# Two prompt tiles of a PEER layer taken through the whole expert table by matrix products, in place of gathered rows

## What is computed

```python
q = (hb @ w_q).reshape(PEER_BLOCK, PEER_HEADS, 2, PEER_KEY_DIM // 2)
# top 16 of 128 on each half, top 16 of their sums: 8 heads x 16 experts e of 16384
gate = jax.nn.softmax(top_s, axis=-1)
act = jax.nn.gelu(jnp.einsum('thkd,td->thk', u_tab[e], hb), approximate=False)
return jnp.einsum('thk,thkd->td', gate * act, v_tab[e])
```

## Time and profile before

| | us |
|---|---|
| median of 3 runs | 3367.15 (3362.72 to 3370.08) |
| span of the profiled execution | 3372.4 |
| TensorE busy | 2967.9 |
| VectorE busy | 2247.2 |
| ScalarE busy | 1569.5 |
| GpSimd busy | 1299.0 |

### The profile page before, as it was taken

One profiled execution on the slowest core, in us unless ns is written; L12 is line 12 of the kernel. 1 busy time (PEld: TensorE's weight loads), 2 busy tenths in 40 slices (PEclk: granted clock), 3 DMA queues, 4 the chain that ended last, 5 costly groups with the idle time before them and its releaser, 6 DMA issues.

```text
span 3372.4 us, 34890 instructions
## 1 busy us (share of the span) xinstructions
PE 2967.9 (88%) x10654; PEld 1563.0 (46%) x10654; DVE 2247.2 (67%) x5353; ACT 1569.5 (47%) x4312; POOL 1299.0 (39%) x1097
## 2 busy tenths in 40 slices
PE   7988899988999898989898888998897988798877
PEld 5764556653445444554454333443353434353322
DVE  1268737685678647884779568866777486873854
ACT  2137334555456334643456345644563454432433
POOL 0023324344344434443434444453334443343532
PEclk8998999999999999999999999999999998899999
DMA  4279999999999999999999999999999989999998
GB/s 175 91 298 362 387 386 396 418 394 421 421 420 411 421 422 419 393 405 422 421 400 413 421 422 421 410 421 422 396 382 408 422 351 333 353 393 369 421 422 342
DMA packets 241250, 1298.74 MB, mean 385 GB/s; under 512 B 46068, under 2 KB 70804, under 8 KB 100646
## 3 DMA queue, kind: packets, MB, share of 16 engines
q0 software_dynamic: 156672, 1140.92, 82.5%
q1 hardware_dynamic: 84390, 155.59, 12.4%
HBM read 1279.41 MB, written 16.44 MB: 384 GB/s over the span
## 4 chain that ended last, share of the span: by engine, by line
PE 44%; DMA 28%; DVE 20%; ACT 4%; issue 2%; SPq 1%; POOL 0%; DVEq 0%; ACTq 0%
PE PS L1096 21%; DMA R<-in_t_uv,idx 18%; DVE R L1746 8%; PE PS L779 7%; DMA R<-in_t_uv,idxS 4%; DMA wring<-in_w_out 3%; PE PS L745 2%; PE PS L1018 2%; PE PS L860 2%; PE PS L859 2%; DVE xb L1757 2%; DMA wring<-in_w_query 2%; PE PS L1045 2%; DVE SC L1712 1%; DVE SC L1709 1%
## 5 line engine op out<-in xcount | busy, mean ns | idle before, releaser
L1096 PE MATMUL PS<-R,diag 128*128 128x512 f32 x3776 | 1821.4, 619 | 200.3 <-ACT diag L1378 173.6
L710 POOL DMA_INDIRECT R<-in_t_uv,idx x1024 | 1234.3, 1205 | 1949.1 <-PE PS L1096 1389.3
L1746 DVE CUSTOM_DVE_ANT_0 R<-R,hb 128x1024 f32<-128x1024 f32 x1088 | 1315.7, 1220 | 726.4 <-DMA R<-in_t_uv,idx 645.3
L1096 PEld LDWEIGHTS PS<-R,diag 128*128 128x128 f32 x3776 | 694.6, 195 | 1077.5 <-issue 635.4
L1369 ACT ACTIVATE acts<-dots 128x1 f32<-128x1 f32 x1088 | 217.2, 200 | 1103.1 <-DVE dots L1746 1100.4
L1378 ACT ACTIVATE diag<-ident,wv 128x128 f32<-128x128 f32 x880 | 353.7, 402 | 76.9 <-PE PS L1096 49.0
L779 PE MATMUL PS<-R 128*128 128x128 f32 (+2 forms) x2272 | 317.1, 295 | 38.6 <-ACT stg L1140 26.7
L779 PEld LDWEIGHTS PS<-R 128*128 128x128 f32 x2272 | 298.5, 196 | 113.1 <-issue 104.5
L1371 ACT ACTIVATE wv<-gate,acts 128x1 f32<-128x1 f32 x1024 | 301.9, 295 | 33.3
L1757 DVE SCALAR_TENSOR_TENSOR xb<-R,wv,xb 128x1024 f32<-128x1024 f32 x144 | 184.4, 1281 | 1.7 <-ACT wv L1371 1.7
L1018 PE MATMUL PS<-wring,T 128*128 128x512 f32 x256 | 133.0, 649 | 42.6 <-DMA wring<-in_w_out 42.6
(11 more groups left out here) (243 smaller groups left out, 2376.0 us busy)
## 6 DMA issues: line engine op xcount, KB each, us to landing
wring<-in_w_out SPq DMA_DIRECT2D x64, 512.0 KB, 14.0
wring<-in_w_query SPq DMA_DIRECT2D x64, 512.0 KB, 8.1
R<-in_t_win SPq DMA_DIRECT2D x38, 512.0 KB, 8.5
R<-in_t_uv,idx POOLq DMA_INDIRECT x1024, 14.0
R<-in_t_win SPq DMA_DIRECT2D x9, 1024.0 KB, 16.0
pr<-prd SPq DMA_DIRECT2D x8, 976.0 KB, 12.7
prd<-stg SPq DMA_DIRECT2D x54, 128.0 KB, 7.6
xb<-in_x_prompt SPq DMA_DIRECT2D x8, 512.0 KB, 7.9
```

Source lines behind the costliest of these rows:

```text
L710: e.indirect_dma_start(dst, None, table, bass.IndirectOffsetOnAxis(ap=index, axis=0)).then_inc(S[s], c.count(name, s, 16))
L1096: m = mm(bank(n), diag[:, NTH[s] % DR, :], pair(s)[:, D + 512 * n:D + 512 * n + 512], start=begins, stop=s == last_slot(t), skip_group_che ...
L1746: e.tensor_tensor_reduce(u, u, hb[:, tile_of(g) % 2, :], 1.0, 0.0, ALU.mult, ALU.add, dots[:, g % NW:g % NW + 1]).then_inc(dve_done, c.cou ...
```

## The change

Tiles 3 and 5 (`DENSE`) no longer have slots. The remaining tiles go in the order `GO`, 832 slots in all. For the dense tiles:

- `gb` (71 steps over 68 slots, twice): for each token of the tile a 128 x 128 matrix of its gates over all 16,384 experts, out of two one-hot matrices that DVE builds (four operations of 128 columns for two tokens) and PE multiplies; ACT copies it to `g_stage`, SP stores it in DRAM (`spread_g`, 8 stores of 1 MB a tile in pieces of 512 bytes).
- `dn` (264 steps over slots 582 to 826): 64 groups of 256 experts. SP loads u transposed (1 MB), v (1 MB) and a quarter of 1 MB of `spread_g`; PE forms u x h for both dense tiles at once (2 x 8 products of 256 columns), ACT applies gelu, DVE multiplies by the gates, PE adds w x v to four PSUM banks (8 products of 512 columns).
- `kept_x`, `kept_h`: residual and h of the dense tiles, stored and loaded again; `fin` ends the two tiles.

Besides: `on_dve` takes two slots of five, the first six of a tile, and all from slot 560 (`PE_END`) on; the ring has eight buffers, from slot 440 (`NARROW`) on seven; each tile's mixers are laid over 66 slots (`BEGIN`), the whole top-k over 40 of them; the input projections lie beside slots 20 to 76 and 112 to 258; the sample's attention beside 492 to 560. `g_final` is no longer loaded for each tile: PE spreads one row into `Y` (`gfin`). `xb`, `hb`, `idx` and `gate` hold three tiles (`OWN`, `PRIOR`). The sample tile's two halves are added by one product with `fold` at the end.

```diff
-RN = 9
+RN = 8
-WIDE = 4 * P + 38, 6 * P + 8
-NSLOT = NTILE * P + NSMP
+GO = [1, 2, 4, 6, 7, 8, SMP]
+DENSE = [3, 5]
+OWN = {1: 1, 2: 0, 3: 2, 4: 1, 5: 2, 6: 0, 7: 2, 8: 1, 9: 0}
+PRIOR = {4: 1, 5: 3, 6: 2, 7: 5, 8: 4, 9: 6}
+NSLOT = P * (len(GO) - 1) + NSMP
+NARROW = 440
+PE_END = 560
+NGRP = P // 2
 def on_dve(s):
-    return s < P * NTILE and 3 <= s % P < 57 and s % P % 3 == 2
+    return s >= PE_END or s % P < 6 or s % 5 in (1, 3)
 def ring():
-        if s == WIDE[0]:
-            free.extendleft(range(RN, RN + 2))
-        if s == WIDE[1]:
+        if s == NARROW:
             free = deque(i for i in free if 2 * i < SAUX)
+BEGIN = {2: 17, 3: 92, 4: 158, 5: 224, 6: 290, 7: 356, 8: 422, SMP: 492}
 def plan():
-    for n, at, end in ((1, 8, 164), (2, 182, 4 * P + 28)):
+    for n, at, items_at, end in ((1, 6, 20, 76), (2, 96, 112, 258)):
         spread(stage("ldx", n), at, at + 1)
+        spread(prep(n), at + 4, items_at - 4)
+        spread(stage("ldw", n), items_at - 4, items_at - 3)
+        spread(stage("items", n), items_at, end)
+    for t in range(2, SMP):
+        at = BEGIN[t]
+        spread(stage("att", t) + stage("ret", t), at, at + 36)
+        spread(stage("ldb", t), at + 18 if t > 2 else 8, at + 19)
+        spread(tail(t), at + 36, at + 58)
+        spread(top(t, 0) + top(t, 1), at + 58, at + 98)
+        if t > 2:
+            spread(stage("ldr", t), at + 24, at + 25)
+        if t + 1 <= NTILE:
+            spread(stage("lda", t + 1), at + 42, at + 43)
+            spread(stage("kv", t + 1) + stage("q", t + 1), BEGIN[t + 1] - 8, BEGIN[t + 1])
+    for j, at in ((0, 262), (1, 334)):
+        spread(stage("gb", j), at, at + 68)
+    at = BEGIN[SMP]
+    spread(stage("ldc", SMP), at - 24, at - 1)
+    spread(stage("lds", SMP), at - 22, at - 16)
+    spread(stage("kv", SMP) + stage("q", SMP), at - 8, at)
+    spread(stage("atts", SMP) + stage("rets", SMP), at, at + 68)
+    spread(stage("ldr", SMP), at + 50, at + 51)
+    spread(tail(SMP), at + 68, at + 90)
+    spread(top(SMP, 0), at + 90, at + 110)
+    spread(stage("sts", SMP), at + 72, at + 92)
+    spread(stage("dn", 0), at + 90, NSLOT - 6)
+    spread(stage("fin", 0) + stage("fin", 1), NSLOT - 6, NSLOT + LAG)
...
@@ SyncE @@
+            def gb(p, j):
+                for f in range(8):
+                    yield from p.to(5 + 8 * f + 8)
+                    at = 8 * j + f
+                    e.wait_ge(act_done, c.at("act", f"G{j}_{8 * f + 7}"))
+                    dma(spread_g.rearrange("(g p) (c x) -> p g c x", p=P, c=16)[:, :, at, :],
+                        g_stage[f % 2].rearrange("p (g x) -> p g x", g=16), f"gs{f % 2}", f"G{j}_{f}")
+            def load_u(i):
+                if i >= 2:
+                    e.wait_ge(pe_done, c.at("pe", f"dU{i - 2}"))
+                dma(d_u[i % 2], A["t_ut"][P * i:P * i + P, :], f"du{i % 2}", f"u{i}")
+            def load_v(i):
+                if i >= 2:
+                    e.wait_ge(pe_done, c.at("pe", f"dV{i - 2}"))
+                for a in range(2):
+                    dma(d_v[i % 2][a], A["t_uv"][2 * P * i + P * a:2 * P * i + P * a + P, D:2 * D], f"dv{i % 2}", f"v{i}_{a}")
...
@@ TensorE @@
+            def dn(p, t):
+                for k in range(4 * NGRP + 4):
+                    yield from p.to(4 + k)
+                    i, what = k // 4, k % 4
+                    if what % 2 == 0 and i < NGRP:
+                        a = what // 2
...
+                        for q in range(NCH):
+                            m = mm(at, u[:, q, P * a:P * a + P], TB[:, :, P * q:P * q + P], start=q == 0, stop=q == NCH - 1,
+                                   skip_group_check=True)
+                    if what % 2 and i:
+                        i, j = i - 1, what // 2
+                        if j == 0:
+                            e.wait_ge(S[f"dv{i % 2}"], c.at(f"dv{i % 2}", f"v{i}_1"))
+                            e.wait_ge(dve_done, c.at("dve", f"dW{i}"))
+                        for n in range(2):
+                            for a in range(2):
+                                m = mm(bank(4 + 2 * j + n), d_w(i)[:, 2 * P * a + P * j:2 * P * a + P * j + P],
+                                       d_v[i % 2][a][:, 512 * n:512 * n + 512], start=i == 0 and a == 0,
+                                       stop=i == NGRP - 1 and a == 1, skip_group_check=True)
...
@@ ScalarE @@
+            def dn(p, t):
+                for i in range(NGRP):
+                    yield from p.to(4 + 4 * i + 3)
+                    e.wait_ge(pe_done, c.at("pe", f"dU{i}"))
+                    if i >= 4:
+                        e.wait_ge(pe_done, c.at("pe", f"dV{i - 4}"))
+                    act(d_w(i), bank(2 + i % 2), ACT.Gelu).then_inc(act_done, c.count(f"dg{i}"))
...
@@ VectorE, its 64 steps @@
+            def gb(p, j):
+                for n in range(64):
+                    yield from p.to(3 + n)
...
+                    if n >= 2:
+                        e.wait_ge(pe_done, c.at("pe", f"G{j}_{n - 2}"))
+                    for tok in range(2):
+                        m = 2 * n + tok
+                        ts(g_hot(n, tok, 0), iota[:], g_kT[:, P + m:P + m + 1], g_kT[:, 2 * P + m:2 * P + m + 1], ALU.is_equal,
+                           ALU.mult).then_inc(dve_done, c.count())
+                        ts(g_hot(n, tok, 1), iota[:], g_kT[:, m:m + 1], None, ALU.is_equal).then_inc(
+                            dve_done, c.count(f"Gh{j}_{n}" if tok else None))
@@ VectorE @@
+            def dn(p, t):
+                for i in range(NGRP):
+                    yield from p.to(4 + 4 * i + 4)
+                    n = i // 4
+                    if i % 4 == 0:
+                        e.wait_ge(S[f"dg{n % 2}"], c.at(f"dg{n % 2}", f"g{n}"))
+                    e.wait_ge(act_done, c.at("act", f"dg{i}"))
...
+                    tt(w, w, g, ALU.mult).then_inc(dve_done, c.count(f"dW{i}"))
...
@@ VectorE @@
+            def fin(p, j):
+                yield from p.to(0)
+                e.wait_ge(S["dx"], c.at("dx", "x1"))
+                e.wait_ge(pe_done, c.at("pe", f"dV{NGRP - 1}"))
+                tt(d_x[j], two(4 + 2 * j), d_x[j], ALU.add).then_inc(dve_done, c.count(f"sd{j}"))
```

More of the change, by code:

```diff
@@ L88 @@
 NTH = {s: i for q in (BY_PE, BY_DVE) for i, s in enumerate(q)}
+PE_OF = {t: [s for s in BY_PE if tile_of(s) == t] for t in GO}
+SUMMED = [t for t in GO if PE_OF[t]]
 def stage(st, t):
@@ L253, in build @@
         prd = nc.dram_tensor("prd", (SMP * P, IN_W), F32).ap()
+        kept_h = nc.dram_tensor("kept_h", (2 * P, D), F32).ap()
+        kept_x = nc.dram_tensor("kept_x", (2 * P, D), F32).ap()
+        spread_g = nc.dram_tensor("spread_g", (P // 8 * P, 2 * D), F32).ap()
         def bank(b, lo=0, hi=512):
@@ L562, in ldc @@
                     e.wait_ge(*spent(c, max(s for s in wide if s in q)))
+                e.wait_ge(pe_done, c.at("pe", "G1_63"))
+                for f in range(2):
+                    e.wait_ge(S[f"gs{f}"], c.at(f"gs{f}", f"G1_{6 + f}"))
                 st_in = A["state_ret"].rearrange("o b (c a) d e -> (o a) d b c e", a=2)
@@ L667, in peer @@
+            def fin(p, j):
+                yield from p.to(3)
+                t = DENSE[j]
+                e.wait_ge(dve_done, c.at("dve", f"yd{j}"))
+                dma(A["o_yp"][P * (t - 1):P * t, :], d_x[j], "yd", f"y{t}")
             def peer(g):
-                for t in range(1, SMP + 1):
+                for t in GO:
                     if g == last_slot(t) + LAG + 3:
@@ L1100, in _, with gfin @@
+            def gfin(t):
+                for n in range(2):
+                    m = mm(bank(n), ones(n), gfin_half(n), start=True, stop=True)
+                m.then_inc(pe_done, c.count(f"gfin{t}"))
             run(dict(prep=prep, items=items, kv=kv, meta=meta, q=q, att=att, ret=ret, atts=atts, rets=rets, out=out, norm2=norm2,
-                     query=query, quart=quart), peer)
+                     query=query, quart=quart, gb=gb, dn=dn), peer)
         @block.scalar
@@ L1763, in build @@
+            run(dict(prep=prep, kv=kv, meta=meta, q=q, att=att, ret=ret, atts=atts, rets=rets, out=out, norm2=norm2, top=top, gb=gb, dn=dn,
+                     fin=fin), peer)
     return new_marks
```

360 lines of the change are left out of this document (251 added, 109 removed).

## The result

| | before | after |
|---|---|---|
| median, us | 3367.72 (3362.72 to 3370.08) | 3591.13 (3584.77 to 3596.5) |
| span of the profiled execution, us | 3372.4 | 3583.0 |

Ratio 1.0661, 95% interval 1.0638 to 1.0683: 6.6% slower. The forecast was 3395 us in a range of 3220 to 3510: the sign was right (slower had a chance of 0.53), the size and the range were not.

A forecast was written before the change was run, and what follows sets the result against it. The kernel before was taken as DMA-bound after its first 190 us, TensorE following at 88%. For the changed kernel, 2376 us to slot 582, 984 dense and 40 at the end gave 3400 of span, forecast 3395, range 3220 to 3510.

The forecast's parts named there:

- heavy stretches: Seven 40-slot stretches with a tile's whole top-k and most of the next attention: VectorE-bound, 144 us each, 1008 in all.
- light stretches: Five 26-slot stretches between heavy stretches, holding the projections: 84 us each by DMA, 420 us in all.
- margin for a bound by DMA alone: 2% that a DMA-bound tile loses, added to the 2054 us from slot 20 on: 41 us.
- dense part: Slots 582 to 826: DMA-bound, 410 MB in 984 us, TensorE 909 us and 4 to 8% behind.
- second rival: Uncovered hand-offs between TensorE, gelu and VectorE in the dense part, 2 us a group: 1058 not 984, total 3470; chance 0.15.
- the 144: VectorE's time in us for one of the heavy stretches: slot products, top-k, kv, q and most of an attention.
- Building G: 40 steps of four 128-column VectorE operations in each of two heavy stretches, 0.19 us an operation: +60 us for both.
- full ring: Five slots of gathers already held when one of the light stretches begins: 12 us less DMA time there.
- the third rival: Three weight buffers, 14.0 us to land, set the light stretches: +11 to 15 us in seven tiles, total 3490; chance 0.08.
- The sample's attention: Slots 492 to 560: 235 us, between 210 at the engines' pace and 290 with the chain unchanged.
- The first rival: Stretches even out and total DMA time is the bound: 3198 us, partly evened up to 3330; chance 0.33.
- 60 where 40 was the full rate: Writing spread_g in 512-byte pieces, 16.8 MB: 60 us of DMA taken, 40 at full rate, most of it hidden.

The follow-up runs named there:

- the denser kernel before: Kernel before, with attention and retention of tiles 3 to 8 over 36 slots, not 49, and projections over 22, not 44: 3521.47 us, ratio 1.0429.

## Why the prediction was right or wrong

| part | forecast | measured |
|---|---|---|
| to slot 20 | 281 | 277 |
| slots 20 to 75 | 245 | 244 |
| 75 to 115 | 151 | 142 |
| 115 to 150 | 110 | 145 |
| three heavy stretches without G | 432 | 459 |
| two with G | 348 | 374 |
| 480 to 520 | 144 | 177 |
| five light stretches | 420 | 521 |
| 520 to 560 | 134 | 137 |
| 560 to 582 | 70 | 92 |
| margin for a bound by DMA alone | 41 | - |
| dense part, 582 to 826 | 984 | 981 |
| end | 40 | 34 |

**Bytes and counts** held, and so did the **dense part**: 981 us at 418 GB/s against 984, TensorE 909.74 us busy against 909. The second rival (hand-offs there) fell; its stretch was below the forecast's.

**The heavy stretches** held in kind: VectorE 90 to 96% busy over their 40 slots, DMA share 0.76 to 0.84. They came out 5 to 12 us above the 144, and those with G together 26 above 348. Building G was mis-sized: L2015 and L2017 took (89.6 + 72.8)/512 = 0.317 us an operation, not 0.19; 512 x 0.127 = 65 us more work on VectorE. The upper bound, 0.276 from the earlier trace rows, was itself too low.

**The step that failed is the rule by which every stretch was priced**, that it takes as long as its most loaded engine, with 2% more where that is DMA. From slot 115 to 480 the forecast had 1310 us (before its margin for DMA) and 1499 were measured. The busy time of the fullest engine, stretch by stretch as in the table, adds up to 1338 us there. So the loads themselves were mis-sized by 28 us in all, and 161 us are time in which no engine was full. The rule held in the dense part, where 64 like groups follow each other, and in the kernel before, where DMA led by far (2506 of 2588 us). It fails where engines at 75 to 95% hand steps to each other in order: with u, v and three quarters of the gathers' bytes gone, five periods still took 1091 us of 1360.

**The largest term of it is the light stretches**, 84 us as 87 and some 9 more of bytes, less 12 for a full ring: they took 104 on average, 101 us too much over five. Bytes are the small part. The five moved 185 MB, which are 440 us at 421 GB/s, where their 420 us hold 177 MB: 20 us. In these 20 two errors nearly cancel, which is luck: the ring gave no credit (gathers were 5 to 7 slots ahead of the u products at both ends of each stretch, and brought 134 MB, 127 slots in place of some 106), and the other loads were put too high. The other 81 us are DMA below its rate, 355 GB/s on average. Some 30 to 34 of them are the weight ring, the third rival, which I had at 11 to 15 us a tile with a chance of 0.08: five buffers shortened the four light stretches that they reach from 422 to 388 us (418 with seven gather buffers alone). Its price was near and its chance too low. The rest, some 50 us, no run took apart.

**Slots 115 to 150 (+35), 480 to 520 (+33) and 560 to 582 (+22)** were priced by the most loaded engine as well. In the first, DMA's bytes were mis-sized: 52.4 MB, 124 us, not 110; and five weight buffers took it from 145 to 133 us (136 with seven gather buffers alone). In the last, TensorE is busy 48 of 92 us and VectorE 56: the tail of the sample tile, step after step. The sample's attention, 68 slots, took 260 us, where I had chosen 235 between 210 and 290: the chain weighed more than I gave it, and most of the +33 is this. No run changed these last two alone, so their causes stay argued.

By differences in the table a tile's 272 us (1360/5) divide into 218 that stay with the mixer steps, 21 for the gathers' bytes, 33 for the u and v products, each on top of those before it. What the 218 consist of was not taken apart further; TensorE is busy for 76 to 83% of them, at a granted clock of 0.83 to 0.85. In slots: from slot 20 to 582 one took 2291/562 = 4.1 us, the forecast had 3.7. DMA alone needs 2.49 for its gather, and 3.1 with the other 140 MB of these slots (729 MB in all).

**The first rival** (stretches even out), a chance of 0.33, fell: DMA share was 0.90, not 0.99, and the denser kernel before alternates between 419 and 315 GB/s.

**Two smaller questions.** Queue 1 took 23.9% of 3583 us against 12.4% of 3372 before: 438 us of 16 engines for 167.8 MB more, where 421 GB/s makes 399. By this estimate, which puts all of the excess on them, the 512-byte pieces of spread_g cost 39 us over the full rate, store and load together; I had 60 where 40 was the full rate of the store, so some 20 too little at most. The Trainium skill ("DMA: Bandwidth & Descriptors", Specifications: 512 B is the smallest transfer at line rate) is not contradicted by that; no run stored them alone. And a gather's issue on GpSimd did not grow beside VectorE's 370 more products: L824 has a mean of 1145 ns, before it was 1297.40/1088 = 1192 ns. Yet an issue is longer beside VectorE: one with no VectorE instruction beside it took 0.94 us on average in both kernels, one that met an instruction with two inputs 1.24 us before and 1.25 after. The mean fell because fewer met one, 549 of 832 against 907 of 1088. The Trainium skill ("GPSIMD Engine Reference", Key points) tells of SBUF interfaces shared with such instructions, and both traces agree.

## What to carry to other kernels

Before work is taken away from the stream that bounds a kernel, ask what that stream covers: here some 355 us of DMA a tile hid 204 to 235 us of mixer steps, and with 66 slots and 203 us of DMA a tile these came to the surface. Price the cover by an experiment that costs one edit of the old kernel, laying the dependent steps at the new density with all else left in place; it cost 144 us, where the whole change cost 223. And the wait for a load among larger ones was shortened more by two more buffers (PEld's for `w_query` from 79.9 to 44.2 us) than by making the load a quarter as large (to 64.5).
